# A two-block transformer kernel on one core: silu of the second block made from the hyperbolic tangent, and ScalarE's root guesses issued one step later

## What is computed

```python
proj = rms_norm(x, norm_g) @ w_in
# q, k are normed per head: q * rsqrt(mean(q*q) + EPS) * gain, then rope
oa = moba_attention(qa, ka, va)        # 6 heads, causal softmax here, 512 tokens
ob = dilated_attention(qb, kb, vb)     # 6 heads, three patterns joined by a mask
om = memory_attention(qm, km, vm)      # 4 heads over 256 memory rows
y = concat([oa * silu(a_g), ob * silu(b_g), om * silu(m_g)], axis=-1)
x = x + y @ w_out
```

## Time and profile before

| what | value |
|---|---|
| median of 3 runs | 2555.38 us |
| the profiled execution: its time, its span | 2561.07 us, 2559.3 us |
| TensorE busy, matmuls | 2463.1 us, 96% of the span |
| ScalarE busy | 1080.3 us, 42% |
| VectorE busy | 1127.0 us, 44% |
| GpSimd busy | 1118.2 us, 44% |
| ACT_TABLE_LOADs on ScalarE | 41, 52.6 us, 1283 ns each |

### The profile page before, as it was taken

The page is one execution under the profiler, slowest core; times in us unless marked ns, Lnnn a source line. Parts: engine busy times, 40 slices in busy tenths (PEclk is TensorE's granted clock), DMA queues, the critical chain, the costliest instruction groups (busy, mean ns, idle before and its releaser), DMA issues.

```text
span 2559.3 us, 30020 instructions
## 1 busy us (share of the span) xinstructions
PE 2463.1 (96%) x10938; PEld 1929.0 (75%) x10938; DVE 1127.0 (44%) x1748; ACT 1080.3 (42%) x1584; POOL 1118.2 (44%) x828
## 2 busy tenths in 40 slices
PE   7999999989999999999999989999999998999988
PEld 6888888667888888888888567888887665776656
DVE  5544115564444105444024645444046655465552
ACT  4333123544333224333132644333135676357772
POOL 4555445315555444555445325555454232343323
PEclk9999999999999999999999999999999999999999
DMA  4222223202222222222223212222233222132221
GB/s 168 84 98 98 99 99 114 83 34 99 98 98 98 88 94 99 98 98 91 90 101 115 80 46 87 98 98 99 99 117 106 81 69 73 50 107 69 80 75 66
DMA packets 37896, 233.24 MB, mean 91 GB/s; under 512 B 5680, under 2 KB 5680, under 8 KB 11184
## 3 DMA queue, kind: packets, MB, share of 16 engines
q1 hardware_dynamic: 36000, 226.51, 25.8%
q10 hardware_dynamic: 1808, 5.51, 0.6%
HBM read 223.62 MB, written 2.10 MB: 88 GB/s over the span
## 4 chain that ended last, share of the span: by engine, by line
issue 59%; POOL 40%; POOLq 1%
POOL w_lo L432 40%; POOLq L426 0%; POOLq L430 0%; POOLq L210 0%; POOLq L432 0%; POOLq L1865 0%
## 5 line engine op out<-in xcount | busy, mean ns | idle before, releaser
L432 POOL TENSOR_TENSOR w_lo<-raw,w_hi 128x512 fp32r<-128x512 f32 x824 | 1117.9, 1389 | 1440.6 <-ACT w_hi L917 1440.5
L440 PE MATMUL ps<-h_hi,w_hi 128*128 128x512 f32 x2304 | 924.7, 401 | 27.8 <-POOL w_lo L432 16.4
L442 PE MATMUL ps<-h_hi,w_lo 128*128 128x512 f32 x2304 | 903.7, 392 | 0.0
L441 PE MATMUL ps<-h_lo,w_hi 128*128 128x512 f32 x2304 | 903.4, 392 | 0.0
L917 ACT ACTIVATE w_hi<-raw 128x1024 fp32r<-128x1024 f32 x412 | 413.2, 1052 | 890.3 <-PE ps L442 889.0
L440 PEld LDWEIGHTS ps<-h_hi,w_hi 128*128 128x128 f32 x2304 | 436.8, 190 | 130.1 <-POOL w_lo L432 18.5
L441 PEld LDWEIGHTS ps<-h_lo,w_hi 128*128 128x128 f32 x2304 | 437.0, 190 | 93.8 <-issue 5.8
L442 PEld LDWEIGHTS ps<-h_hi,w_lo 128*128 128x128 f32 x2304 | 436.1, 189 | 93.0
L442 PE MATMUL ps<-hid_hi,w_lo 128*128 128x512 f32 x704 | 280.9, 399 | 0.0
L441 PE MATMUL ps<-hid_lo,w_hi 128*128 128x512 f32 x704 | 277.4, 394 | 0.0
L440 PE MATMUL ps<-hid_hi,w_hi 128*128 128x512 f32 x704 | 276.0, 392 | 0.0
(11 more groups left out here) (237 smaller groups left out, 2066.9 us busy)
## 6 DMA issues: line engine op xcount, KB each, us to landing
raw<-in_stream SPq DMA_DIRECT2D x206, 1024.0 KB, 4.8
hraw<-xs SPq DMA_DIRECT2D x96, 64.0 KB, 2.0
x_sb<-in_x SPq DMA_DIRECT2D x4, 512.0 KB, 7.8
out_x<-x_sb SPq DMA_DIRECT2D x8, 256.0 KB, 2.7
mem_sb<-in_mem ACTq DMA_DIRECT2D x1, 1024.0 KB, 12.7
rec_sb<-in_recip ACTq DMA_DIRECT2D x2, 512.0 KB, 4.8
memn<-in_mem ACTq DMA_DIRECT2D x1, 1024.0 KB, 5.7
dist_sb<-in_dist ACTq DMA_DIRECT2D x2, 448.0 KB, 3.6
```

The lines of the kernel that those rows point to most:

```text
L432: gp.tensor_tensor(w_lo[:, s, c], raw[:, s, c], w_hi[:, s, c].bitcast(F32), ALU.subtract).then_inc(lo_split, 1)
L440: pe.matmul(dst, l_hi, r_hi, start=first, stop=False)
L441: pe.matmul(dst, l_hi, r_lo, start=False, stop=False)
L442: return pe.matmul(dst, l_lo, r_hi, start=False, stop=last)
```

## The change

The gate is stored halved, ScalarE makes `tanh` of it instead of `silu`, into `sq[:, 1, :]`, and a new VectorE instruction completes (1 + tanh(g/2)) * (g/2) in step 6, ahead of `head_norm`. The root guesses are no longer issued in step 4 but in step 5, behind the scaling of unit 2 (the stage's third unit) and behind the tanh. The memory stage's own double-width silu (L1163) stays as it is. The wait for the mean squares stands ahead of the tanh.

```diff
@@ ScalarE, attention_step
-                if here and s == 4 and not here.last:
-                    act.wait_ge(hn_ms, 2 * (GROUPS * here.l + here.gi + 1) + 2)
-                    pair_guesses(T)
                 if here and s == 5 and not here.last:
                     act.wait_ge(gate_raw, 7 * here.l + here.gi + 1)
                     gate = y[:, here.gi - 1, :]
-                    act.activation(gate, gate, ACT.Silu).then_inc(g_in, 1)
+                    act.wait_ge(hn_ms, 2 * (GROUPS * here.l + here.gi + 1) + 2)
+                    act.activation(sq[:, 1, :], gate, ACT.Tanh).then_inc(g_in, 1)
+                    pair_guesses(T)
@@ VectorE, attention_step
                 if here and s == 6 and not here.last:
+                    gate = y[:, here.gi - 1, :]
+                    dve.wait_ge(g_in, 7 * here.l + here.gi + 1)
+                    dve.scalar_tensor_tensor(out=gate, in0=sq[:, 1, :], scalar=1.0, in1=gate, op0=ALU.add, op1=ALU.mult)
                     head_norm(T, (-0.125, 1.0), qk)
@@ VectorE, producer
-                        dve.tensor_tensor(y[:, gi - 1, :], ps[:, 7 if more else 6, :], scale2[:], ALU.mult).then_inc(gate_raw, 1)
+                        dve.scalar_tensor_tensor(out=y[:, gi - 1, :], in0=ps[:, 7 if more else 6, :], scalar=0.5,
+                                                 in1=scale2[:], op0=ALU.mult, op1=ALU.mult).then_inc(gate_raw, 1)
```

## The result

The change makes the kernel slower, by 8 to 10 us where 14.5 were forecast.

What follows compares the result with a forecast made beforehand. TensorE, busy 96% of the span, was taken as the bound, so only its waits and clock could change. Pair stages 8.5, stage 6 3.1, stage 1 2.4 and clock 0.5 gave +14.5 us: 2570 us, range 2564 to 2578.

Steps and rivals of the forecast that it cites:

- The maximum of unit 3 behind the Newton step: Pair stages: VectorE's queue holds unit 3's exponential until 2029.55 instead of 2028.66; each stage ends 1.06 us later, 8.5 in all.
- the new wait before the scores: Pair stages: TensorE's next scores wait for VectorE's head norms, about 0.4 us beyond the old start, 0.8 us of waiting.
- the reciprocal behind the head norms without idle time: Pair stages, VectorE: unit 3's reciprocal starts behind the head norms at 2031.27 instead of 2030.21, 1.06 us later.
- the one long idle stretch in stage 6: Stage 6: TensorE idles some 6 us until the head norms; the whole stage costs 1.5 us, 3.1 for both layers.
- the sum's silence on stage 7: Stage 7: stage 6's delay is passed on through the wait for w_lo; nothing was added or taken off behind it.
- the price of unit 3's transposes: Stage 6: after the long idleness the clock is lower, so the transposes' 1.09 us grow by about 0.5.
- The guesses' delay: Pair stages, ScalarE: scaling 1.11 us plus tanh 0.63 us go first, so guesses and Newton step come 1.74 us later.
- Stage 1: Unit 5's transposes come 1.2 us later, 2.4 us for both layers, plus half a microsecond for a possible clock drop.
- The added instruction: VectorE, ahead of the head norms: costs 0.60 to 0.61 us in a row, bounds 0.6 and 0.7.
- The rival by which ScalarE's chain decides: Unit 3's maximum does not hold the exponential, which starts 1.2 us earlier; 11 us faster, 2544 us; chance 0.05.
- The rival of two delays that cancel: Short tanh and hidden added instruction leave the time within 5 us of the old; chance 0.05.
- The rival of a clock that falls in every stage: TensorE's short gaps lower its clock, each of ten stages losing up to 1.7 us: 2587 us; chance 0.08 in full.

Runs made afterwards that it cites:

- mask first: The change with VectorE doing unit 3's mask and maximum ahead of the Newton step; ratio to the kernel before 0.9975, median 2550.26 us.
- tanh only: The change with the root guesses back in step 4, keeping tanh and the added VectorE instruction; ratio to the kernel before 0.9976, median 2551.97 us.
- its second trace: The kernel before, run again with no edit; ratio 0.9996, median 2559.11 us.
- The order of stage 6 alone: The kernel before with the root guesses in step 5, ahead of the silu, in stage 6 only; ratio 0.9986, median 2552.62 us.
- The change's second trace: The change, run again with no edit; ratio to the kernel before 1.0026, median 2564.24 us.
- mask first and gate late: The change with VectorE's Newton step behind unit 3's mask and the added instruction moved to step 7; ratio to before 0.9945, median 2542.76 us.
- the first four experiments: The unedited kernel before, the change with guesses in step 4, before with guesses in step 5, the change with its added instruction late: 0.9996, 0.9976, 0.9995, 1.0024.

## Why the prediction came out as it did

**In the pair stages the mechanism was right.** The maximum of unit 3 behind the Newton step, the new wait before the scores, the reciprocal behind the head norms without idle time, the one long idle stretch in stage 6: all of it is in the trace, and undoing the queue alone (mask first) or the guesses' place alone (tanh only) turns the loss into a gain of 0.25%. Stage 2's new waits were forecast at 0.8 and 0.95 us and are 0.57 and 0.95, stage 1's at about 1.9 and 0.9 and are 1.89 and 0.81.

**The step that failed** is the sum's silence on stage 7: it passed stage 6's delay on unchanged and put nothing, without a reason, for what comes behind the wait for w_lo. There the change gave back 5.0 us in its first trace and 7.2 in its second, against the first trace of before. The time is gained where the clock is higher. In the kernel before, TensorE was at full clock when it came to that wait of 3.55 us; the clock then fell, and the panel's matmuls ran at half of it. The window behind that wait in the first trace of before, then in its second trace; then, in the change's first trace, the window around unit 3's transposes of stage 6 and the two behind the first wait for w_lo in either layer:

```profile
2170.31:2175.31 5.00, 5.00 (x12) 0.50 0.64 210
```

```profile
2163.36:2168.36 5.00, 5.00 (x12) 0.50 0.62 210
```

```profile
2161.00:2166.00 5.00, 3.04 (x14) 0.50 0.00 0
2172.78:2177.78 5.00, 5.00 (x18) 0.68 0.63 210
2498.12:2503.12 5.00, 5.00 (x26) 1.00 0.58 210
```

In the change the clock had fallen in the 6.27 us of idleness, was at 1.2 GHz while little was to be done (the transposes grew from 1.09 to 1.97 us), and was back for the panel in layer 1. In layer 0 it fell once more in the wait of 2.01 us, but came back sooner than before. The low stretch has moved from where TensorE is the bound to where it mostly waits. The order of stage 6 alone, which changes nothing else, shows that the place of these guesses does it: 188.0 us instead of 193.1 to 193.9, and 3.6 us by the ratio of many runs.

Only part of the 5.0 us lies behind the first wait, though: 3.2 us come between its end and the end of the second wait for w_lo (37.20 and 37.24 us became 36.40 and 34.89), 1.8 us behind the second. That second wait is 3.5 us long in all twelve traces, and the same work stands ahead of it, yet the clock behind it differs; before, then the change's first trace:

```profile
2207.51:2212.51 5.00, 5.00 (x12) 0.50 0.58 210
2528.26:2533.26 5.00, 5.00 (x12) 0.50 0.59 213
```

```profile
2209.18:2214.18 5.00, 5.00 (x15) 0.66 0.59 210
2533.01:2538.01 5.00, 5.00 (x15) 0.66 0.62 213
```

The change's second trace has 0.50 and 1.00 there, and the tanh alone, with the guesses in step 4, has 0.50 and 1.00 too. No idleness close ahead of that wait explains this, so for the 1.8 us the cause of the higher clock stays open. Over all traces the stretch took 193.1, 193.9, 193.5 and 190.9 us with the guesses in step 4, and 186.6 to 191.1 us in eight traces with stage 6's guesses in step 5, so the two groups just touch. The forecast had looked at this clock only for the price of unit 3's transposes. It put 0.5 us a layer; the transposes grew by 0.88 us, since the whole of them ran at the lower level, and the stretch from their start to the end of the wait by 0.7 and 1.1. That the median, 2565.31 us, still lies within the stated range is luck: nothing in the range was set aside for a gain in stage 7.

**A term was mis-sized.** The guesses' delay was taken as 1.11 + 0.63 = 1.74 us. From the copies of the values to the Newton step it was 2023.72 - 2019.56 = 4.16 us (the copies' row stands just ahead of the earlier trace rows in the trace), and is 2022.94 - 2017.24 = 5.70, so 1.54. The scaling begins 0.53 us after copies of 0.63 us, and the tanh 1.02 us after scalings of 1.12: an activation starts 0.1 us before its predecessor ends, while a table load starts only when all is done. So the scalings and the tanh, put ahead of the load, each add their length less 0.1 us, where the forecast added their lengths in full. The Trainium skill, ScalarE: Activation LUTs, section "What ACT_TABLE_LOAD costs", states that activations back to back overlap by about 93 ns; the trace agrees. With 1.54 the stage comes to 0.86 instead of 1.06 us, and 0.81 is measured: 2.0 us of the sum over eight stages.

**The rest.** Stage 1 was forecast at 1.2 us a layer and took 1.1; the clock stayed up there (1.00 from 1991 to 1997 us), so the half microsecond for it was too much. The added instruction took 0.69 us, 0.60 in a row, as the head norms did. The mean of the same kind of instruction with one of its tensors in PSUM is 686 ns as well (128x512, 64 times, in the page's part 5), so the trace shows no half rate for two float32 tensors in SBUF. The rival by which ScalarE's chain decides fell, for the change as made; with the condition that the prediction gave for it, the maximum ahead of the Newton step, both versions are faster than before. Its gain was put at 0.70 us a stage and 11 us in all; mask first and gate late together gained 0.79 us and 14. The rival of two delays that cancel fell with the 0.81 us. The rival of a clock that falls in every stage fell too: in all twelve traces the granted clock stayed at its higher level from the start of the second block to stage 6 of layer 0.

## What to carry to other kernels

Removing work from an engine that is only 42% busy helps where it stands on a chain, and the same edit can lengthen a chain through another engine: ask what the moved instruction releases, and what is queued behind that on the engine that waits. When a wait moves or grows on TensorE, look at the clock behind it too: here it fell in a wait of 6.27 us and was partly back before the work that is bound by it. And of two halves of a change, try each alone: here one was worth -0.24% and the other, harmless by itself, took it all back and more. Halves need not add: a stage changed by -0.34 and +0.16 us for them alone, and by +0.81 for both.

## What was not expected

- A clock that falls early in a wait can be cheaper than one that falls late: with stage 6's guesses one step later, stage 6 was 0.2 us longer a layer and the layers' ends came 5.1 to 5.9 us sooner in the trace (3.6 us by the ratio of many runs). Which of the windows stays low varied from run to run; the rule behind it stays open. The tanh alone, with the guesses in step 4, had one stretch of 190.9 us, 2 to 3 us less than its kind.
- Two executions of the untouched first block differ by up to 7 us in when the second block begins. Over its 35 runs beside the first four experiments, the kernel before took 2550.0 to 2561.4 us. Part of it goes with the clock: by the traces' rows of the granted clock, the first block had about 7 us at the lower level in the two traces where it ended first (1947.3 and 1947.4) and about 14 us in the two where it ended last (1953.9 and 1954.2), which is worth at most half of that difference. The rest was not tried. The prediction widened its range by 3 us for this, from three runs of before.
